# ScalarE copies half of the selected key blocks, VectorE multiplies the copies in place

## The chip, the cores and the metric

One core of one Trainium2 chip runs the kernel. The metric is the device time of one execution in microseconds (us), and less is better. All durations below come from one profiled execution of the kernel before.

## What is computed

One layer of a hybrid decoder is computed for a prompt of 512 positions and, beside it, for 8 decode sequences with one new token each and 4,096 cached positions. The projections, the gated MLP half and the prompt's attention are the large matmul part. The change lies in the decode attention, cut here to what matters (`moba_sample` of the reference):

```
k_full = cache_k[page_table].reshape(Bd, n_full, 256, H, D)     # 16 blocks of 256 keys
kmean  = mean(k_full, axis=2)
gate   = einsum('bhtd,bnhd->bhtn', q, kmean)
_, sel = top_k(gate, 3)                                         # 3 blocks for each head
kg, vg = keys and values of the selected blocks                 # 8 heads x 3 = 24 blocks
s      = einsum('bhtd,bhtkd->bhtk', q, kg) * scale - slope * distance
p      = softmax(s);  out = einsum('bhtk,bhtkd->bhtd', p, vg)
```

Every number is float32.

## The kernel before

**Order.** Each engine executes a list of steps whose order is written at build time by a planner (`make_plan`, line 51). The planner keeps lanes of steps for each engine, with a planned duration and the steps that each depends on, and takes the next step by start time and then by lane rank. Two of its settings matter here. `MARGIN` (line 397) is a hold: on TensorE, a step of the lanes gate, score and spread is planned no earlier than its inputs' planned time plus this hold, so that TensorE gets projection work in front of it. On the chip only the order is left of the plan; each step then waits on semaphores for its real inputs.

**TensorE** (PE) carries the projections of the prompt (line 1036, seven chunks of the input projection; line 1142, the output projection), the prompt attention (lines 1090 to 1120) and, put between them, the small decode steps: `gs` (line 1159) sums the key rows of four blocks, `bc`, `mt` and `mb` (lines 1166, 1171, 1175) spread numbers over partitions, `pv0` and `pv1` (line 1188) multiply probabilities by values.

**One decode sequence b (batch), 8 in a row.**
- GpSimd (POOL) issues 16 gathers of key blocks from the cache into the tile K (line 899), with up to 5 in flight. K holds exactly one sequence. So the first gather of sequence b+1 (line 973) waits until the selected blocks of b have been taken out of K.
- VectorE (DVE) adds the two rows of each block (`ks`, line 744) and TensorE sums them (`gs`).
- VectorE computes the block scores and the top three (`ga`, lines 1572 to 1589).
- `ex` (lines 1608 to 1628) is split in PARTS = 4 parts of 6 instructions. Each instruction reads one 128x128 piece of K (one head's two halves of one block, at an address that comes from registers loaded from selT), multiplies it by q (tile qb), and writes it to kq, which lies in the tile ksum. The last one signals `s_ext`.
- `pg` (lines 1590 to 1607) looks up the page numbers and signals `s_sel`. It stands behind the first part of `ex`, for the last sequence ahead of all of them.
- `sr` (line 1634) reduces kq over the head dimension to scores and signals `s_scr`.
- `bc`, `mt`, `mb` add distances, take the maximum and exponentiate (ScalarE, line 1356), then TensorE executes `pv0` and `pv1`.
- The values V are fetched by SyncE's queue (SP) and by POOL's behind the 16 key gathers of b+1, for the last sequence by SP, POOL and ScalarE's queue (line 729, called by line 1353). All of these fetches wait for `s_sel`.
- SP spreads q of the next sequence over the partitions into qb (line 824), after `s_ext`.

**ScalarE** (ACT) evacuates the projections from PSUM (line 1302), does the exponentials (line 1339) and the copies of transposed probabilities (line 1347) of the prompt attention, sums of squares (line 1237), the copies behind `pv` (lines 1382 and 1383), and issues the weight loads (line 655). It does nothing with K.

## Time and profile before

| What | Value |
|---|---|
| Time, median of 3 runs | 459.38 us (459.01 to 478.45) |
| Time of the profiled execution | 457.99 us |
| Its span in the profile | 456.4 us |
| PE busy | 402.1 us (88%) |
| DVE busy | 278.8 us (61%) |
| POOL busy | 244.7 us (54%) |
| ACT busy | 125.2 us (27%) |

The span runs from the first to the last record of the profile; the time has 1.6 us more around it. PE's busy time includes the waiting of pipelined matmuls behind one another, so 88% says that it is seldom without work, not that it is at its peak. An engine's idle time costs something only where another engine, or the end, waits for it.

### The profile page before, as it was taken

To read this page: it belongs to the slowest core of one execution; us is meant where nothing else is said; L and a number is where in the kernel's file an instruction comes from. 1 tells how busy PE (TensorE), PEld (TensorE's weight loads), DVE (VectorE), ACT (ScalarE), POOL (GpSimd) and SP (SyncE) were. 2 spreads that over 40 slices of the span, in tenths; PEclk is the share of its full clock that TensorE was granted. 3 is DMA by queue.
4 is the path that set the end of the run, shared out by engine and by line. 5 is a ranking of instruction groups with operands and counts; after the bars stand their busy time and mean duration, and the time that the engine had idled before them with its cause. 6 is when DMAs were issued, how large, how long until landed. Compare 5 with 4: busy or idle time off the path is not lost.

```text
span 456.4 us, 8864 instructions
## 1 busy us (share of the span) xinstructions
PE 402.1 (88%) x2696; PEld 189.5 (42%) x2696; DVE 278.8 (61%) x756; ACT 125.2 (27%) x282; POOL 244.7 (54%) x347
## 2 busy tenths in 40 slices
PE   4896997998779999899998897989999388999993
PEld 2543442433343444344553354434443253334433
DVE  2443167447624569666966884868865796567432
ACT  2310120000012223554547522362435401000101
POOL 4776305556446506563377745882566556667121
PEclk9897998999979999899999998999999769999999
DMA  8999158996799936997499849975699599945311
GB/s 223 408 390 337 49 183 227 363 328 164 202 382 331 254 105 190 361 320 185 117 336 318 241 127 333 327 202 156 210 368 337 162 362 378 343 103 117 115 46 52
DMA packets 79695, 111.26 MB, mean 244 GB/s; under 512 B 46560, under 2 KB 47584, under 8 KB 79648
## 3 DMA queue, kind: packets, MB, share of 16 engines
q0 software_dynamic: 22576, 71.45, 46.4%
q1 hardware_dynamic: 45280, 21.26, 18.3%
q10 hardware_dynamic: 11792, 17.98, 13.2%
q8 instruction: 22, 0.36, 0.3%
q14 instruction: 25, 0.20, 0.1%
HBM read 106.34 MB, written 4.29 MB: 242 GB/s over the span
## 4 chain that ended last, share of the span: by engine, by line
PE 27%; DMA 25%; issue 13%; POOL 10%; DVE 9%; SPq 7%; another core or an unknown queue 4%; DVEq 2%; POOLq 2%; ACT 1%
DMA K<-in_cache_k,kidx 20%; PE PA L1036 12%; POOL K L899 8%; PE PA L1142 7%; SPq L777 4%; DVE ksum L1619 4%; DMA V<-in_cache_v 2%; PE SB L990 2%; PE GB L1159 2%; DMA V<-in_page_table 2%; PE DC L1188 1%; DVEq L1617 1%; POOLq L726 1%; SPq L780 1%
## 5 line engine op out<-in xcount | busy, mean ns | idle before, releaser
L899 POOL DMA_INDIRECT K<-in_cache_k,kidx x128 | 135.5, 1059 | 135.3 <-DVE ksum L1619 69.2
L1036 PE MATMUL PA<-wbuf,hT 128*128 128x512 f32 x384 | 187.8, 623 | 4.5 <-ACT vn L1302 2.6
L744 DVE TENSOR_TENSOR ksum<-K 128x512 f32<-128x512 f32 x128 | 86.5, 689 | 74.7 <-DMA K<-in_cache_k,kidx 54.4
L1036 PEld LDWEIGHTS PA<-wbuf,hT 128*128 128x128 f32 x384 | 69.4, 196 | 82.1 <-issue 73.3
L729 POOL DMA_DIRECT2D V<-in_cache_v x128 | 76.2, 595 | 33.8 <-issue 26.1
L1142 PE MATMUL PA<-wbuf,hT 128*128 128x512 f32 x128 | 59.6, 606 | 0.0
L1619 DVE TENSOR_TENSOR ksum<-K,qb 128x128 f32<-128x128 f32 x192 | 41.8, 287 | 10.9 <-issue 4.3
L1159 PE MATMUL GB<-ksum,win 128*32 128x512 f32 x256 | 34.1, 604 | 5.0 <-DVE ksum L744 4.7
L1142 PEld LDWEIGHTS PA<-wbuf,hT 128*128 128x128 f32 x128 | 23.1, 192 | 25.7 <-issue 25.2
L1036 PE MATMUL PA<-hT,wbuf 128*128 128x512 f32 x64 | 31.0, 630 | 0.0
L990 PE MATMUL SB<-wbuf,hTs 128*32 128x128 f32 x576 | 22.0, 305 | 6.7 <-DMA wbuf<-in_w_in 3.7
L1634 DVE TENSOR_REDUCE sc<-ksum 128x48 f32<-128x3072 f32 x8 | 26.8, 3352 | 0.2
L1339 ACT ACTIVATE pr<-pr,smax 128x128 f32<-128x128 f32 (+3 forms) x32 | 18.0, 561 | 31.8 <-DVE smax L1518 20.6
L990 PEld LDWEIGHTS SB<-wbuf,hTs 128*32 128x32 f32 x576 | 18.4, 123 | 12.0 <-issue 7.0
L1515 DVE SCALAR_TENSOR_TENSOR pr<-alibi,SB 128x128 f32<-128x128 f32 (+3 forms) x32 | 15.4, 482 | 11.2 <-PE SB L1090 10.1
L912 POOL TENSOR_SCALAR rstd<-msum 128x1 f32<-128x1 f32 (+1 forms) x18 | 4.8, 268 | 26.7 <-DVE msum L1545 20.0
L1302 ACT ACT_TABLE_LOAD x13 | 16.7, 1283 | 8.2 <-PE PA L1036 6.6
L1188 PE MATMUL DC<-V,pex 128*32 128x64 f32 x768 | 15.5, 229 | 3.2 <-DMA V<-in_cache_v 2.8
L1347 ACT COPY pT<-SB 128x128 f32<-128x128 f32 (+3 forms) x32 | 12.8, 422 | 19.3 <-PE SB L1099 12.7
L1036 PEld LDWEIGHTS PA<-hT,wbuf 128*128 128x128 f32 x64 | 12.1, 199 | 14.4 <-issue 14.4
L1237 ACT ACTIVATE junk<-PA 128x512 bf16<-128x512 f32 x8 | 4.8, 595 | 45.4 <-PE PA L1142 39.1
L1518 DVE TENSOR_REDUCE smax<-pr 128x1 f32<-128x128 f32 (+3 forms) x32 | 15.6, 486 | 1.1
(200 smaller groups left out, 363.5 us busy)
## 6 DMA issues: line engine op xcount, KB each, us to landing
wbuf<-in_w_in ACTq DMA_DIRECT2D x20, 512.0 KB
V<-in_cache_v SPq DMA_DIRECT2D x240, 32.0 KB
V<-in_cache_v POOLq DMA_DIRECT2D x128, 32.0 KB, 2.8
wbuf<-in_w_out ACTq DMA_DIRECT2D x8, 512.0 KB
wbuf<-in_w_in SPq DMA_DIRECT2D x8, 256.0 KB, 8.6
K<-in_cache_k,kidx POOLq DMA_INDIRECT x128, 7.8
wbuf<-in_w_in SPq DMA_DIRECT2D x4, 512.0 KB
qb<-q_rows SPq DMA_DIRECT2D x8, 256.0 KB
```

What stands on the lines that cost most here:

```text
L729: eng.dma_start(V[j * ROWS:(j + 1) * ROWS, h * TOP + k, :, :], v_pages[bass.ds(page, 1), :, :, h * HD:(h + 1) * HD] .rearrange("a p r d -> ...
L744: eng.tensor_tensor(ksum[:, n % SUMS, :], K[:, n, 0, :], K[:, n, 1, :], ALU.add).then_inc(s_dsum, 1)
L777: sp.dma_start(dst, src, allow_slow_non_contiguous=True).then_inc(s_small, 16)
L899: pool.indirect_dma_start(K[:, n, :, :].rearrange("p r w -> p (r w)"), None, k_rows, bass.IndirectOffsetOnAxis(ap=kidx[:, b, n:n + 1], axis=0)
L990: last = pe.matmul(bank[32 * j:32 * j + 32, :], hTs[:, kc, :], w[:, kc, j * P:(j + 1) * P], start=(kc == 0), stop=(kc == KC - 1), tile_pos ...
L1036: last = pe.matmul(bank[:, :], lhs, rhs, start=(kc == 0), stop=(kc == KC - 1))
L1142: last = pe.matmul(bank[:, :], hT[:, kc, t * P:(t + 1) * P], wbuf[:, c % 2, kc, :], start=(kc == 0), stop=(kc == KC - 1))
L1159: last = pe.matmul(GB[32 * j:32 * j + 32, :], win[:, 31 - g:63 - g], ksum[:, (4 * g + j) % SUMS, :], start=(g == 0), stop=(g == G - 1), ti ...
L1188: last = pe.matmul(DC[32 * j:32 * j + 32, hh * HD:(hh + 1) * HD], pex[:, h, i, r:r + 1].broadcast_to([P, 32]), V[:, h * TOP + i, r, :], st ...
L1339: act.activation(pr[:, a % 2, 0:(i + 1) * P], pr[:, a % 2, 0:(i + 1) * P], ACT.Exp, bias=smax[:, a % 2:a % 2 + 1], accum_out=ssum[:, h, i: ...
L1619: last = dve.tensor_tensor(kq[:, h * TOP + k, :, :], K[:, bass.ds(n, 1), :, h * HD:(h + 1) * HD] .rearrange("p a r d -> p (a r) d"), qb[:, ...
L1634: dve.tensor_reduce(sc[:, :, :, :].rearrange("p h k r -> p (h k) r"), kq[:, :, :, :], AX.X, ALU.add).then_inc(s_scr, 1)
```

## The change

For every sequence, the pieces are numbered x = 8k + h (k the rank of the block, h the head). The first 12 (`BY_ACT`: rank 0 of all heads and rank 1 of heads 0 to 3) are now taken out of K by ScalarE, as plain copies into kq. The other 12 are taken by VectorE as before, in four parts of 3. Then a new VectorE step `em` multiplies the copied pieces by q in place, in two instructions (8 pieces and 4 pieces). `sr` waits for it. The next sequence's gathers wait for VectorE's pieces and ScalarE's copies; the spread of q waits for `em` too. ScalarE's copies start after `s_sel`, so behind `pg`. In the planner they have the first lane of ScalarE and a planned duration of 4.9 us, `ex` goes from 1.7 to 0.9 for a part, `em` gets 1.9, and MARGIN goes from 0.6 to 1.0.

```diff
-PARTS = 4
+PARTS, BY_ACT = 4, 12
...
-("ACT", "weight square score exp turn sample side evacuate squares fetch"),
+("ACT", "copyk weight square score exp turn sample side evacuate squares fetch"),
...
-            deps = [("DVE", ("ex", b - 1, PARTS - 1))] if b else []
+            deps = [("DVE", ("ex", b - 1, PARTS - 1)), ("ACT", ("ex", b - 1))] if b else []
...
-        for s in ([("pg", b)] + parts if b == B - 1 else parts[:1] + [("pg", b)] + parts[1:]) + [("sr", b)]:
+        for s in ([("pg", b)] + parts if b == B - 1 else parts[:1] + [("pg", b)] + parts[1:]) + [("em", b), ("sr", b)]:
             deps = [("ACT", ("mb", b - 1))] if s[0] == "sr" and b else []
-            add("DVE", "gate", s, {"ex": 1.7, "pg": 1.2, "sr": 3.4}[s[0]], *deps)
+            if s[0] == "em":
+                deps.append(("ACT", ("ex", b)))
+            add("DVE", "gate", s, {"ex": 0.9, "pg": 1.2, "em": 1.9, "sr": 3.4}[s[0]], *deps)
+        add("ACT", "copyk", ("ex", b), 4.9, ("DVE", ("pg", b)))
         if b:
-            add("SP", "spread", ("qb", b), 3.0, ("DVE", ("ex", b - 1, PARTS - 1)))
+            add("SP", "spread", ("qb", b), 3.0, ("DVE", ("em", b - 1)))
...
-TILE_US, KEY_US, LAG, MARGIN, SLACK, QUARTERS = 7.4, 1.65, 0.25, 0.6, 0.05, 8
+TILE_US, KEY_US, LAG, MARGIN, SLACK, QUARTERS = 7.4, 1.65, 0.25, 1.0, 0.05, 8
...
                         sp.wait_ge(s_ext, b)
+                        sp.wait_ge(s_exm, b)
...
                         pool.wait_ge(s_ext, b)
+                        pool.wait_ge(s_exa, b)
...
+                elif kind == "ex":
+                    b = s[1]
+                    act.wait_ge(s_sel, b + 1)
+                    if b >= 1:
+                        act.wait_ge(s_scr, b)
+                    for x in range(BY_ACT):
+                        k, h = divmod(x, H)
+                        if h == 0:
+                            block_regs = [act.alloc_register(f"ablk{b}_{k}_{i}") for i in range(H)]
+                            act.load(block_regs, selT[k:k + 1, b % 2, 0:H])
+                        n = act.snap(block_regs[h], min_val=0, max_val=NB - 1)
+                        last = act.copy(kq[:, h * TOP + k, :, :],
+                                        K[:, bass.ds(n, 1), :, h * HD:(h + 1) * HD].rearrange("p a r d -> p (a r) d"))
...
+                    last.then_inc(s_exa, 1)
...
-                    size = H * TOP // PARTS
-                    for x in range(size * part, size * (part + 1)):
+                    size = (H * TOP - BY_ACT) // PARTS
+                    for x in range(BY_ACT + size * part, BY_ACT + size * (part + 1)):
...
+                elif kind == "em":
+                    b = s[1]
+                    dve.wait_ge(s_exa, b + 1)
+                    by_rank = kq[:, :, :, :].rearrange("p (h k) r d -> p k h r d", k=TOP)
+                    q_heads = qb[:, :].rearrange("p (h d) -> p h d", h=H)
+                    for k in range(-(-BY_ACT // H)):
+                        hs = min(H, BY_ACT - k * H)
+                        last = dve.tensor_tensor(by_rank[:, k, 0:hs, :, :], by_rank[:, k, 0:hs, :, :],
+                                                 q_heads[:, 0:hs, :].unsqueeze(2).broadcast_to([P, hs, 2, HD]),
+                                                 ALU.mult)
+                    last.then_inc(s_exm, 1)
                 elif kind == "sr":
                     b = s[1]
                     dve.wait_ge(s_ext, b + 1)
+                    dve.wait_ge(s_exm, b + 1)
```

## Rows read from the trace of the kernel before

**Rows 1.** The page: busy time of each engine, and the chain by line.

```profile
PE 402.1 (88%) x2696; PEld 189.5 (42%) x2696; DVE 278.8 (61%) x756; ACT 125.2 (27%) x282; POOL 244.7 (54%) x347
...
DMA K<-in_cache_k,kidx 20%; PE PA L1036 12%; POOL K L899 8%; PE PA L1142 7%; SPq L777 4%; DVE ksum L1619 4%; DMA V<-in_cache_v 2%; PE SB L990 2%; PE GB L1159 2%; DMA V<-in_page_table 2%; PE DC L1188 1%; DVEq L1617 1%; POOLq L726 1%; SPq L780 1%
```

**Rows 2.** Windows of 15 us: busy us, (instructions), then PEclk, DMA share, GB/s.

```profile
360.00:375.00 15.00, 8.43 (x73) 6.12 (x74) 13.89 (x40) 3.05 (x10) 7.59 (x8) 0.59 0.88 306
...
420.00:435.00 15.00, 15.00 (x132) 6.88 (x131) 6.20 (x18) 2.22 (x9) 3.15 (x7) 1.00 0.36 103
```

**Rows 3.** Waits of POOL and PE: who waited for whom, total us, times, longest.

```profile
POOL K L899 <- DVE ksum L1619: 69.2, 7, 19.9
...
PE DC L1183 <- DMA V<-in_cache_v: 5.0, 1, 5.0
PE GB L1159 <- DVE ksum L744: 4.7, 7, 1.3
...
PE SB L1128 <- DVE yb L1471: 2.3, 1, 2.3
```

**Rows 4.** Timeline of sequence 1: start, us, engine, line, what.

```profile
111.52 1.30 DVE L1619 TENSOR_TENSOR ksum<-K,qb 128x128 f32<-128x128 f32 x6 [0.79 <-DVE selT L1589]
...
113.87 0.20 DVE L1607 STREAM_TRANSPOSE selT<-selw 32x32 int32<-32x32 int32 x1
...
114.23 0.49 DVE L1619 TENSOR_TENSOR ksum<-K,qb 128x128 f32<-128x128 f32 x2 [0.16 <-DVE selT L1607]
...
115.17 3.55 DVE L1619 TENSOR_TENSOR ksum<-K,qb 128x128 f32<-128x128 f32 x16 [0.45 <-issue]
...
118.75 3.35 DVE L1634 TENSOR_REDUCE sc<-ksum 128x48 f32<-128x3072 f32 x1
...
118.99 1.01 POOL L899 DMA_INDIRECT K<-in_cache_k,kidx  x1 [6.55 <-DVE ksum L1619]
...
129.41 0.68 DVE L744 TENSOR_TENSOR ksum<-K 128x512 f32<-128x512 f32 x1
```

**Rows 5.** Timeline of the last sequence: from selection to ScalarE's value fetches and `pv1`.

```profile
408.30 0.20 DVE L1607 STREAM_TRANSPOSE selT<-selw 32x32 int32<-32x32 int32 x1
...
409.46 6.41 ACTq L729 DMA_DIRECT2D V<-in_cache_v  x8
...
416.85 6.14 ACTq L729 DMA_DIRECT2D V<-in_cache_v  x8
...
431.23 0.86 PE L1188 MATMUL DC<-V,pex 128*32 128x64 f32 x46
```

**Rows 6.** Timeline of ACT: small copies from PSUM; small activations that read SBUF.

```profile
155.66 0.43 ACT L1347 COPY pT<-SB 128x128 f32<-128x128 f32 x2 [1.57 <-PE SB L1099]
...
218.16 0.31 ACT L1237 ACTIVATE junk<-vn 128x128 bf16<-128x128 f32 x1
218.38 0.19 ACT L1237 ACTIVATION_READ_ACCUMULATOR junk<-vn 128x1 f32 x1
```

**Rows 7.** DVE by form: count, busy us, mean ns, idle before.

```profile
L744 DVE TENSOR_TENSOR ksum<-K 128x512 f32<-128x512 f32 x128 | 86.5, 689 | 74.7 <-DMA K<-in_cache_k,kidx 54.4 <-PE GB L1159 13.6 <-issue 4.4
```

**Rows 8.** Timeline at 367 us: POOL's gathers beside VectorE's two-input instructions.

```profile
367.66 1.35 POOL L899 DMA_INDIRECT K<-in_cache_k,kidx  x1 [3.07 <-DVE ksum L1619]
369.31 1.56 POOL L899 DMA_INDIRECT K<-in_cache_k,kidx  x1 [0.30 <-issue]
371.18 0.94 POOL L899 DMA_INDIRECT K<-in_cache_k,kidx  x1 [0.30 <-issue]
...
367.29 2.73 DVE L1471 SCALAR_TENSOR_TENSOR yb<-yb,rstd,vn 128x512 f32<-128x512 f32 x4
```

**Rows 9.** Timeline: what ACT and PE do around the selections of sequences 4 and 6.

```profile
267.80 1.28 ACT L1302 ACT_TABLE_LOAD   x1 [5.77 <-PE PA L1036]
...
362.34 0.63 ACT L1237 ACTIVATE junk<-yb 128x512 bf16<-128x512 f32 x1
...
364.30 0.17 PE L1183 MATMUL DC<-psm,one 128*1 128x8 f32 x1 [4.95 <-DMA V<-in_cache_v]
```

More of the change, by code:

```diff
@@ L63, in add @@
         needs[eng, s] = deps
-    for eng, names in (("PE", "gate score first attention side sample project"), ("ACT", "weight square score exp turn sample side evacuate squares fetch"),
+    for eng, names in (("PE", "gate score first attention side sample project"), ("ACT", "copyk weight square score exp turn sample side evacuate squares fetch"),
                        ("DVE", "first " + DVE_LANES), ("POOL", POOL_LANES), ("SP", "spread rows fetch gather"),
@@ L592, in hymba_kernel @@
         s_scr = sem("selected_k_scored")
+        s_exa = sem("selected_k_copied")
+        s_exm = sem("copied_k_times_q")
         s_mxr = sem("decode_max_ready")
@@ L1353, in _ @@
                     fetch_v(act, b, hh, [k], "va")
+                elif kind == "ex":
[11 more added lines that the diff above has]
+                                        K[:, bass.ds(n, 1), :, h * HD:(h + 1) * HD].rearrange("p a r d -> p (a r) d"))
+                        if h == H - 1 or x == BY_ACT - 1:
+                            for r in block_regs:
+                                act.free_register(r)
+                    last.then_inc(s_exa, 1)
                 elif kind == "mb":
@@ L1611, in _ @@
                         dve.wait_ge(s_sel, b + 1)
-                    size = H * TOP // PARTS
-                    for x in range(size * part, size * (part + 1)):
+                    size = (H * TOP - BY_ACT) // PARTS
+                    for x in range(BY_ACT + size * part, BY_ACT + size * (part + 1)):
                         k, h = divmod(x, H)
-                        if h == 0:
+                        if h == 0 or x == BY_ACT:
                             block_regs = [dve.alloc_register(f"blk{b}_{k}_{i}") for i in range(H)]
```

## The prediction

> **What bounds the kernel now.** I read the page first, then the windows, then the waits, then the timelines around the selections. The page shows two strands [rows 1]. TensorE is busy 402.1 of 456.4 us, and the chain that ended last runs through the key gathers (20% on their DMAs, 8% on POOL's issues) and the projections (12% and 7%), in turns. Neither bounds the kernel alone. The waits show why the change aims where it does [rows 3]: POOL stood 69.2 us in 7 waits for VectorE's last extraction, the longest 19.9 us. K has a single copy, so each of these 7 waits ends in a gather that can't start earlier, and it takes from 118.99 to 129.41 us until VectorE adds its first block [rows 4]. An earlier release moves the whole next sequence. But TensorE waits little for it: 4.7 us in 7 waits for key sums, 5.0 us once for values [rows 3]. And after the last selection at 408.3 us TensorE is filled with output projection (15.00 of 15 us in the window from 420) [rows 2, 5]. So a microsecond gained on the key loop isn't a microsecond at the end. It comes out only as far as it takes idle time off TensorE, which has some 54 us of it (456.4 - 402.1), much at the two ends. The fattest place in the middle is the window from 360: 8.43 of 15 us busy, clock granted 0.59 [rows 2].
>
> **Release of K, today.** In sequence 1 the first 6 pieces take 1.30 us, `pg` ends at 114.07 (113.87 + 0.20), and 2 and 16 more pieces end at 118.72: 4.65 us after the selection is ready [rows 4]. A piece costs 1.30 / 6 = 0.217 us.
>
> **Release of K, after.**
> - The part ahead of `pg` falls from 6 to 3 pieces: 3 x 0.217 = 0.65 us earlier for everything behind it, values included (not in the last sequence, where `pg` stands first).
> - VectorE's rest: 9 pieces and one register load. The first piece came 0.16 us after `pg`, and the register load cost 0.45 us [rows 4]: 0.16 + 0.45 + 9 x 0.217 = 2.6 us after the selection. So ScalarE sets the release.
> - ScalarE's start: in the last sequence its queue's first instruction came at 409.46, 0.96 us after the selection at 408.50, with the same loads of 8 registers from selT [rows 5].
> - Twelve copies: the trace has no ScalarE instruction on K. Bounds: two copies of this size from PSUM took 0.43 us, 0.215 each; an activation that reads 128x128 from SBUF takes 0.31 us, and the engine took its next instruction 0.22 us after its start [rows 6]. Low end 12 x 0.215 = 2.6, high end, nothing overlapped, 12 x 0.31 = 3.7. I take 11 x 0.22 + 0.31 = 2.7, since this row reads SBUF as the copies do. The second register load adds 0 to 0.45 us; I take 0.45.
> - Sum: 0.96 + 2.7 + 0.45 = 4.1 us after the selection (3.6 to 5.1), against 4.65. With the 0.65, the release is 1.2 us earlier (0.2 to 1.7).
>
> *A rule on small operands.* The activation's duration is 0.31 us [rows 6]. The Trainium skill (VectorE: DVE Perf Modes, section The TRN2 errata) gives a ScalarE instruction with SBUF source 224 + 128 = 352 cycles of 1.2 GHz, 0.29 us, and advises tiles of 512 elements and more, which speaks against twelve copies of 128. The duration agrees with the trace; if the fixed part lay bare between all of them, an estimate from that page is 12 x 0.29 = 3.5 us, a release 4.9 us after the selection, and a gain of 0.4 us instead of 1.2.
>
> **What eats at the 1.2 us.** (a) ScalarE is in order. At the selection of sequence 4 it is idle (until 267.80), near that of sequence 6 it is in squares until 362.97 [rows 9]. I take 0.3 us on the mean. (b) `em` now runs beside POOL's first gather. It has two SBUF inputs. Beside four such instructions of VectorE two gathers took 1.35 and 1.56 us, alone the next took 0.94 [rows 8]. `em` ends after about 1.8 us, so it covers one and a bit: +0.4 us (0 to 1.0, for both). Today `sr`, with one input, stands there, and the gather took 1.01 [rows 4]. Left: 1.2 - 0.3 - 0.4 = 0.5 us for each of 7 handovers, 3.5 us by the last sequence (-8 to +12 from the bounds).
>
> *The port rule.* The gather beside two-input work took 1.35 us against 0.94 [rows 8]. The Trainium skill (SBUF — State Buffer, section SBUF: two separate sides) says that VectorE with two SBUF inputs and a GpSimd operation that reads SBUF exclude each other for the whole instruction. The trace shows a slower gather, not one held for all of 2.73 us.
>
> (c) MARGIN grows by 0.4, so TensorE's last `gs` of each sequence is put up to 0.4 us later. The planned release is 6.8 + 1.2 = 8.0 us behind `ga` today and 0.9 + 1.2 + 0.25 + 4.9 = 7.25 after. In the order TensorE's steps thus move 0.35 us earlier for each sequence while the real release moves 0.5: TensorE should wait less for key sums.
>
> **The score path.** 8 pieces are 1024 columns, 4 are 512. A 512-column instruction of this kind takes 0.689 us [rows 7]; two of these bound the first, 1.38 us, less about 0.1 to 0.2 for one start instead of two: `em` 1.2 + 0.7 = 1.9 us. `sr` then ends 4.1 + 0.1 + 1.9 + 3.35 = 9.45 us after the selection, today 4.65 + 3.35 = 8.0 [rows 4]. With 0.65 off it's 0.8 us later. Behind the waiting `em` on VectorE stand `sr`, then maxima of the prompt attention and `bc`. The next key sums are no victim: the first came at 129.41, 7 us after `sr` ended at 122.1 [rows 4]. The plan counts the path 1.4 us longer, so TensorE's order allows for it: cost 0, and up to 5 x 0.8 = 4 us if the five sequences beside the attention aren't covered. VectorE's own load: -12 x 0.217 + 1.9 = -0.7 us per sequence, on an engine busy 61% [rows 1]: 0. SP's spread of q is needed a whole loading phase later: 0.
>
> **The last sequence.** ScalarE copies before it issues its two value fetches, which took 6.41 and 6.14 us from 409.46 and 416.85 [rows 5]. The start moves by 4.1 - 0.96 = 3.1 us, so the second ends near 426 instead of 423, and `pv1` uses the values at 431.23 [rows 5]: hidden by the 5 us, less the landing. Without that cover, one for one.
>
> **The sum at the end.** TensorE's 7 waits for key sums hold 4.7 us; with 0.4 more hold each I take off 7 x 0.4 = 2.8. Its 4.95 us for values at 359 to 364 [rows 9] shrink with the earlier key phase, since POOL fetches those values behind the gathers: real minus planned shift is 6 x (0.5 - 0.35) = 0.9. Against that, near sequence 6 the squares that open the way to the output projection (TensorE waited 2.3 us for it [rows 3]) may stand behind ScalarE's copies: 0 or 3.1 us, I take 0.7. Net -2.8 - 0.9 + 0.7 = -3.0. The profiled execution took 457.99 us (span 456.4 and 1.6 around it), so 455.0; the median of the runs is 1.4 above this execution, so **456**.
>
> **The rivals.**
> - *No gain at the end, 458 to 462.* Copies at their high bound and ScalarE late by half a microsecond leave -0.6 us per handover. For it: TensorE is full behind the last selection. Chance 0.21. In it lies the port rule in full: `em`'s longer instruction holding every first gather costs 1.2 - 0.4 = 0.8 more on each of 7, 455 + 6 = 461. Against: only 0.4 is seen [rows 8]. Chance 0.05 of its own.
> - *Slower, 467 to 476.* ScalarE's copies block the prompt attention. Its exponentials, copies and evacuations stand behind a wait for the selection, and TensorE's order has them at planned times. Each microsecond by which the selection is later on the chip than in the plan, beyond the softness of two PSUM banks, is TensorE idle in sequences 2 to 6: 5 x 2 to 3.5 us = 10 to 17, and the clock falls as at 360 (0.59) [rows 2]. It decides from about 2 us lateness on. Against: VectorE, in order too, waits at the same places today. Chance 0.16.
> - *A large gain, 445 to 450.* The order of TensorE around 358 to 372 comes out free of its waits: 5.0 for values and 2.3 for `yb` [rows 3] and the slow clock, with the 2.8: some 10 us. Chance 0.16.
> - The forecast, 452 to 458: 0.42.
>
> **How the numbers follow.** The likeliest gives 456. About 2% either way (450.2 and 468.6) is what a measurement of this kernel can tell. Faster by more: the large gain, 0.16. Slower by more: most of the blocking case, 0.13. Within: 0.71. The range 447 to 467 leaves out about 0.07 below and 0.13 above.
>
> **What would show it.** The copies 0.20 to 0.24 us apart, from about 1 us behind the selection; the first gather 4.1 us behind it and 1.2 to 1.5 us long; POOL's wait now for ScalarE's line; PE's waits for key sums below 3 us; PE busy again near 402. Copies 0.3 us apart, PE waiting for `pr` or `pT` of ScalarE by more than 5 us, or the key loop shorter by 7 us and more with an end that follows it, would make the prediction wrong.

## The result: 5.4% slower

The changed kernel took 488.27 us (median of 4 runs, 484.39 to 493.04), the kernel before beside it 460.03 us (median of 4 runs). The ratio is 1.054, with a 95% interval from 1.049 to 1.059. The profiled execution took 484.61 us, its span is 483.0. All ratios in this document are of executions whose clock was not disturbed, a median is of all runs, and the profiled executions of e2, e4, e5, e7, e8, e9, e11 and e17 were among the disturbed, longer ones.

Busy time by engine and the group of ScalarE's copies, from the page of the changed kernel (its line numbers are shifted: 1372 is ScalarE's copies, 1643 VectorE's pieces, 1660 `em`, 1670 `sr`, 905 the key gathers, 749 `ks`, 1166 `gs`, 1195 `pv`, 997 the projections of the new tokens):

```profile
PE 409.8 (85%) x2696; PEld 194.0 (40%) x2696; DVE 272.8 (56%) x676; ACT 139.5 (29%) x374; POOL 244.5 (51%) x347
...
L1372 ACT COPY ksum<-K 128x128 f32 x96 | 20.1, 294 | 33.8 <-DVE selT L1631 33.6
```

Waits of the changed kernel (who waited for whom, us in total, times, longest):

```profile
POOL K L905 <- ACT ksum L1372: 75.5, 6, 21.3
...
PE DC L1195 <- issue: 10.1, 13, 1.3
PE SB L997 <- DMA wbuf<-in_w_in: 7.3, 1, 7.3
PE DC L1062 <- ACT junk L1244: 6.8, 2, 6.1
PE PA L1043 <- ACT vn L1309: 6.3, 1, 6.3
...
PE GB L1166 <- DVE ksum L749: 1.5, 2, 1.0
```

TensorE is busy 7.7 us more than in [rows 1] and idle 18.9 us more (73.2 against 54.3). The wait for key sums shrank from 4.7 us [rows 3] to 1.5, as forecast. In its place stand waits that were shorter before: 10.1 us of "issue" between small matmuls of `pv` (before 0.4), 7.3 for weights (3.7), 6.1 at the end (0.8) and 6.3 for `vn` (2.6).

The handover itself went nearly as predicted. Timeline of sequence 1 in the changed kernel:

```profile
111.46 0.20 DVE L1631 STREAM_TRANSPOSE selT<-selw 32x32 int32<-32x32 int32 x1
...
112.58 2.09 ACT L1372 COPY ksum<-K 128x128 f32 x10 [1.63 <-DVE selT L1631]
112.66 1.71 DVE L1643 TENSOR_TENSOR ksum<-K,qb 128x128 f32<-128x128 f32 x8 [0.54 <-issue]
...
114.58 0.49 ACT L1372 COPY ksum<-K 128x128 f32 x2
115.10 1.83 DVE L1660 TENSOR_TENSOR ksum<-ksum,qb 128x1024 f32<-128x1024 f32 x2 [0.74 <-ACT ksum L1372]
115.86 1.35 POOL L905 DMA_INDIRECT K<-in_cache_k,kidx  x1 [7.42 <-ACT ksum L1372]
...
117.02 3.35 DVE L1670 TENSOR_REDUCE sc<-ksum 128x48 f32<-128x3072 f32 x1
```

The selection is ready at 111.66, the last copy ends at 115.07 (3.4 us later), the gather starts at 115.86 (4.2 later; before, 118.99 - 114.07 = 4.9 [rows 4]). So the handover gained, and the span lost 26.6 us (483.0 - 456.4). What follows is about that difference.

A table from the timelines helps to see where. Ahead of the first selection the first keys are loaded. Between the first selection and the last (seven sequences) the time divides into three: selection to first gather, start of the first to start of the last gather (the loading phase), and last gather to the next selection (landing, last additions and `gs`, block scores). The tail is from the last selection to the end.

| profiled execution | to first selection | selection to gather | loading phases | last gather to selection | tail | TensorE idle in the loading phases |
|---|---|---|---|---|---|---|
| before | 66.0 | 35.0 | 175.6 | 131.9 | 47.9 | 18.0 |
| changed | 62.2 | 32.3 | 194.2 | 142.6 | 51.7 | 34.8 |
| e3, new work, old order | 61.3 | 30.0 | 182.5 | 134.6 | 48.3 | 20.6 |
| e17, before, 4 in flight | 59.4 | 35.0 | 204.4 | 121.2 | 49.4 | 27.0 |
| e18, changed, 4 in flight | 60.4 | 33.3 | 203.7 | 112.6 | 51.5 | 18.7 |
| e15, before, 3 in flight | 65.1 | 35.0 | 233.2 | 109.0 | 48.4 | 29.7 |
| e16, changed, 3 in flight | 63.9 | 32.2 | 236.2 | 109.9 | 50.8 | 28.3 |
| e5, half gathers, 5 in flight | 59.5 | 35.0 | 145.4 | 220.8 | 47.6 | 40.9 |
| e13, half gathers, 2 in flight | 69.8 | 35.0 | 229.0 | 99.0 | 51.2 | 22.4 |

Of the 18.9 us that TensorE is idle more in the changed kernel, 16.8 come in the loading phases (34.8 against 18.0) and 7.7 in the tail (15.4 against 7.7), while the rest of the span has 5.6 less.

### The profile page after: what moved, and what is told of

Read it like the earlier page. It is cut to its first block and busy times, and to the rows that moved or that the text cites. A ratio compares the mean times of both kernels' runs of the same rounds, so it can differ in the third digit from the quotient of the medians.

```text
span 483.0 us, 8906 instructions
## 1 busy us (share of the span) xinstructions
PE 409.8 (85%) x2696; PEld 194.0 (40%) x2696; DVE 272.8 (56%) x676; ACT 139.5 (29%) x374; POOL 244.5 (51%) x347
## 5 line engine op out<-in xcount | busy, mean ns | idle before, releaser
L749 DVE TENSOR_TENSOR ksum<-K 128x512 f32<-128x512 f32 x128 | 85.9, 687 | 59.4 <-DMA K<-in_cache_k,kidx 46.0
L997 PE MATMUL SB<-wbuf,hTs 128*32 128x128 f32 x576 | 27.5, 331 | 12.9 <-DMA wbuf<-in_w_in 7.3
L1372 ACT COPY ksum<-K 128x128 f32 x96 | 20.1, 294 | 33.8 <-DVE selT L1631 33.6
L997 PEld LDWEIGHTS SB<-wbuf,hTs 128*32 128x32 f32 x576 | 21.6, 134 | 20.1 <-issue 10.5
L1043 PE MATMUL PA<-hT,wbuf 128*128 128x512 f32 x64 | 29.6, 602 | 0.0
L1195 PE MATMUL DC<-V,pex 128*32 128x64 f32 x768 | 17.7, 221 | 13.4 <-issue 10.1
L1643 DVE TENSOR_TENSOR ksum<-K,qb 128x128 f32<-128x128 f32 x96 | 21.7, 287 | 11.4 <-DVE selT L1613 4.8
L1195 PEld LDWEIGHTS DC<-V,pex 128*32 128x32 f32 x768 | 13.3, 109 | 19.8 <-issue 19.7
L1354 ACT COPY pT<-SB 128x128 f32<-128x128 f32 (+3 forms) x32 | 13.1, 423 | 27.5 <-PE SB L1106 16.8
L1675 DVE TENSOR_TENSOR sbias<-DC,slope 128x24 f32<-128x24 f32 x8 | 1.4, 181 | 34.1 <-PE DC L1173 18.9
L1539 DVE SCALAR_TENSOR_TENSOR pr<-alibi,SB 128x128 f32<-128x128 f32 (+3 forms) x32 | 15.4, 481 | 6.8 <-PE SB L1097 6.7
L1043 PEld LDWEIGHTS PA<-hT,wbuf 128*128 128x128 f32 x64 | 11.4, 190 | 13.8 <-issue 13.7
```

Of the source, the lines that this page charges most:

```text
L749: eng.tensor_tensor(ksum[:, n % SUMS, :], K[:, n, 0, :], K[:, n, 1, :], ALU.add).then_inc(s_dsum, 1)
L997: last = pe.matmul(bank[32 * j:32 * j + 32, :], hTs[:, kc, :], w[:, kc, j * P:(j + 1) * P], start=(kc == 0), stop=(kc == KC - 1), tile_pos ...
L1043: last = pe.matmul(bank[:, :], lhs, rhs, start=(kc == 0), stop=(kc == KC - 1))
L1195: last = pe.matmul(DC[32 * j:32 * j + 32, hh * HD:(hh + 1) * HD], pex[:, h, i, r:r + 1].broadcast_to([P, 32]), V[:, h * TOP + i, r, :], st ...
L1372: last = act.copy(kq[:, h * TOP + k, :, :], K[:, bass.ds(n, 1), :, h * HD:(h + 1) * HD].rearrange("p a r d -> p (a r) d"))
L1643: last = dve.tensor_tensor(kq[:, h * TOP + k, :, :], K[:, bass.ds(n, 1), :, h * HD:(h + 1) * HD] .rearrange("p a r d -> p (a r) d"), qb[:, ...
```

## The experiments

### The order against the work: e1 to e4 and e8

The change does two things at once. It moves work from VectorE to ScalarE, and through MARGIN and new planned durations it makes the planner write another order: 140 of TensorE's 465 steps stand elsewhere. e3 gives the planner the old numbers and the new steps no duration, so that all engines keep the old order with the new steps put in (on SyncE, one spread of q and one fetch change places). e4 keeps the new order and does the old work in it.

**e1**, MARGIN alone, in the kernel before:

```diff
-TILE_US, KEY_US, LAG, MARGIN, SLACK, QUARTERS = 7.4, 1.65, 0.25, 0.6, 0.05, 8
+TILE_US, KEY_US, LAG, MARGIN, SLACK, QUARTERS = 7.4, 1.65, 0.25, 1.0, 0.05, 8
```

> The kernel before with MARGIN 1.0 instead of 0.6; no other edit, so only the order of steps changes. The changed kernel took 488.27 us against 460.03 (ratio 1.054). Theory O (the order that the planner writes is what costs the time, and the hold is the part of it that counts): 475 us or more. Theory W (the new work itself, ScalarE's copies and VectorE's second pass, costs it): 460, within 1% of before. A third reading, O2 (the order counts, but through the planned durations of the new steps): also near 460 here.

Measured 466.86 us (461.63 to 476.79), ratio 1.016 (0.997 to 1.036). It moved 137 of TensorE's steps, and its loss can't be told from none. Theory O, which put the loss on the hold, wanted 475 or more.

**e2**, the changed kernel with the old MARGIN of 0.6:

> The changed kernel with MARGIN back at 0.6. Theory O (hold): 460 or less. Theory W (the work): stays near 488. O2 (any new order is a draw of its own): anywhere from 460 to 500, with other waits of TensorE than in the changed kernel.

Measured 499.28 us (495.04 to 514.25), ratio 1.084 (1.065 to 1.104): worse than the changed kernel. MARGIN 1.0 isn't what made the changed kernel slow.

**e3**, the new work in the old order:

```diff
-TILE_US, KEY_US, LAG, MARGIN, SLACK, QUARTERS = 7.4, 1.65, 0.25, 1.0, 0.05, 8
+TILE_US, KEY_US, LAG, MARGIN, SLACK, QUARTERS = 7.4, 1.65, 0.25, 0.6, 0.05, 8
-            add("DVE", "gate", s, {"ex": 0.9, "pg": 1.2, "em": 1.9, "sr": 3.4}[s[0]], *deps)
+            add("DVE", "gate", s, {"ex": 1.7, "pg": 1.2, "em": 0.0, "sr": 3.4}[s[0]], *deps)
-        add("ACT", "copyk", ("ex", b), 4.9, ("DVE", ("pg", b)))
+        add("ACT", "copyk", ("ex", b), 0.0, ("DVE", ("pg", b)))
```

> The changed kernel's work in the order of before: the planner gets MARGIN 0.6, 1.7 us for each part of VectorE's extraction and 0.0 for ScalarE's copies and VectorE's second pass, which leaves the order of TensorE, ScalarE, VectorE and GpSimd exactly that of before with the new steps put in. Theory W (the work costs it): 485 to 490, as in the changed kernel. Theory O (the order costs it): 452 to 460, that is what was predicted for the work, with the key release after the selection at some 3.5 us against 4.65.

Measured 461.06 us (453.52 to 466.83); the kernel before beside it 463.46.

**e4**, the old work in the new order: the changed kernel, in which `range(BY_ACT)` of the copies and the range of `em` are empty, VectorE takes all 24 pieces, and the waits for `s_exa` and `s_exm` and those of ScalarE's copy step are gone.

> The order of the changed kernel with the work of before: VectorE takes all 24 pieces with q, ScalarE's copy step and VectorE's second pass issue nothing, and their waits are gone. Theory W: back at 460. Theory O: 480 or more, since the order stays. If the work helps and the order harms, this one is the slowest of the four, some 3 to 7 us above the changed kernel.

Measured 484.52 us (477.95 to 488.28), ratio 1.046 (1.024 to 1.068). Busy time on the two pages, first e3, then e4:

```profile
PE 402.9 (88%) x2696; PEld 188.4 (41%) x2696; DVE 272.6 (60%) x676; ACT 144.3 (32%) x378; POOL 244.6 (54%) x347
```

```profile
PE 411.8 (85%) x2696; PEld 194.2 (40%) x2696; DVE 277.3 (57%) x756; ACT 119.2 (24%) x278; POOL 242.2 (50%) x347
```

**e8**, e3 once more with more runs:

> The new work in the old order once more, in 5 rounds, for an interval. Seven handovers of K, each some 0.9 us earlier after the selection. If the gain came through in full: 453 to 455 (ratio 0.985). If TensorE's fixed order swallows it: within 0.5% of before.

Measured 466.40 us (458.79 to 474.68, 12 runs), ratio 1.015 (1.003 to 1.026).

The four corners: old work, old order 460 to 463; new work, old order 461 to 466; old work, new order 485; new work, new order 488. TensorE's busy time points the same way (402.1 and 402.9 against 409.8 and 411.8), but says less: in e8, the same kernel as e3, it is 407.1. **The order costs some 21 to 27 us, the work 0 to 1.5%.** That the handover's gain didn't come through shows in e3's row of the table: 5.0 us less from selection to gather, 6.9 us more in the loading phases and 2.7 more behind them.

### Is it this order, or any other? e7, e9 and e10

**e7** and **e9** change one planned duration of the kernel before by 0.1 us. Every instruction is the same, and 122 and 110 steps of TensorE move.

```diff
-            add("DVE", "gate", s, {"ex": 1.7, "pg": 1.2, "sr": 3.4}[s[0]], *deps)
+            add("DVE", "gate", s, {"ex": 1.8, "pg": 1.2, "sr": 3.4}[s[0]], *deps)
```

> The kernel before with one planned duration changed: 1.8 instead of 1.7 us for each part of the extraction. The same instructions on every engine, in another order (122 of TensorE's 465 steps move). If the order of before is a lucky or tuned draw, and any other costs: 470 to 490. If only the order that came with the change is bad: 456 to 466.

Measured 477.49 us (469.68 to 478.08); the kernel before beside it 462.82.

> The kernel before, in which only the planner's duration of one part of ex goes from 1.7 to 1.6 us; every instruction is the same, and 110 of TensorE's 465 steps stand elsewhere. Theory O (the order that the kernel before has is a good draw, and any plan that differs moves some hundred steps and loses what that draw had): slower, 466 to 485 us where the kernel before is near 460, ratio 1.015 to 1.05. Rival P (what costs is a longer plan for the handover, as in the changed kernel, where the planned release moved; a plan with a shorter part is no loss): ratio 0.99 to 1.01.

Measured 485.84 us (475.47 to 486.69); before beside it 463.02. Neither run has an interval. Lowest against lowest, e7 stands 3.9% above the kernel before beside it (469.68 against 452.03) and e9 4.5% (475.47 against 454.99). Shorter or longer, both lose, so it isn't the direction in which the planned release moved. Nor does every other order lose: e1 moved 137 steps and lost nothing that can be measured.

**e10** gives the changed kernel's planner what its trace shows:

```diff
-            add("DVE", "gate", s, {"ex": 0.9, "pg": 1.2, "em": 1.9, "sr": 3.4}[s[0]], *deps)
+            add("DVE", "gate", s, {"ex": 0.7, "pg": 1.2, "em": 1.9, "sr": 3.4}[s[0]], *deps)
-        add("ACT", "copyk", ("ex", b), 4.9, ("DVE", ("pg", b)))
+        add("ACT", "copyk", ("ex", b), 3.2, ("DVE", ("pg", b)))
```

> The changed kernel, in which the planner gets the durations that its trace shows: 3.2 us for ScalarE's copies instead of 4.9, 0.7 for a part of ex instead of 0.9, MARGIN 1.0 as it was. Theory O (the order is a draw; truer durations by a microsecond or two are no cure, since the plan doesn't know what the chip loses): 470 to 495 us, with no reason to lie below the changed kernel's 485 by more than the spread between draws (some 10 us). Rival T (the order is bad because the plan holds the copies to be 1.7 us longer than they are): back to 458 to 465.

Measured 483.51 us (478.81 to 487.26), ratio 1.061 (1.048 to 1.074). Truer durations are no cure.

Does the plan know? In part. Its own end is 425.9 us for the kernel before and 427.3 for e1, 432.2 for e7, 437.3 for e2, 442.8 for e9: the last three are longer in the plan too. But it holds the changed kernel at 427.9 and e10 at 425.9, and these two should have taken what the kernel before takes, not 24 to 28 us more. Something that the plan doesn't hold hits these orders.

### What hits them: pauses and late signals beside the gathers

In the changed kernel the loading phase of sequence 4 takes 37.2 us (before 25.3). There matmuls of `pv` come singly, with gathers of POOL between them. The timeline of the changed kernel:

```profile
224.52 0.99 PE L1195 MATMUL DC<-V,pex 128*32 128x64 f32 x38
...
224.86 0.93 POOL L905 DMA_INDIRECT K<-in_cache_k,kidx  x1 [0.30 <-issue]
...
226.09 0.94 POOL L905 DMA_INDIRECT K<-in_cache_k,kidx  x1 [0.30 <-issue]
226.67 0.27 PE L1195 MATMUL DC<-V,pex 128*32 128x64 f32 x2 [1.16 <-issue]
...
227.34 0.94 POOL L905 DMA_INDIRECT K<-in_cache_k,kidx  x1 [0.30 <-issue]
...
228.18 0.22 PE L1195 MATMUL DC<-V,pex 128*32 128x64 f32 x1 [1.24 <-issue]
228.58 0.93 POOL L905 DMA_INDIRECT K<-in_cache_k,kidx  x1 [0.30 <-issue]
...
230.34 0.26 PE L1195 MATMUL DC<-V,pex 128*32 128x64 f32 x1 [1.22 <-issue]
...
237.63 0.15 ACT L1406 COPY denr<-DC 1x8 f32<-1x8 f32 x1 [9.64 <-remote]
```

38 matmuls take 0.99 us together, and the next eight take 9.2 us. "issue" says that the profile shows nothing they wait for. Their last one ended at 234.7, and ScalarE's copy of the result started at 237.63.

Signals come late too. In the same kernel, three transposes of `pr` (line 1106) end at 288.72, and ScalarE's copy of them starts at 297.15, after 7.3 us of idle time that ends with a signal ("remote"); POOL issues gathers until 296.25; a spread (line 1173) ends at 293.34 and VectorE's `sbias` starts at 297.30. TensorE then waited 6.35 us for `vn`, which stood behind that copy:

```profile
288.23 0.49 PE L1106 MATMUL SB<-ident,pr 128*128 128x128 f32 x3
...
292.94 0.40 PE L1173 MATMUL DC<-spread,one 8*128 8x24 f32 x2
...
297.15 0.48 ACT L1354 COPY pT<-SB 128x384 f32<-128x384 f32 x1 [7.30 <-remote]
297.30 0.18 DVE L1675 TENSOR_TENSOR sbias<-DC,slope 128x24 f32<-128x24 f32 x1 [5.80 <-remote]
...
299.68 2.08 PE L1043 MATMUL PA<-wbuf,hT 128*128 128x512 f32 x2 [6.35 <-ACT vn L1309]
```

The ends of matmuls are modelled in these profiles, so it isn't told apart whether the signal was late or the matmul itself.

It isn't new. In the kernel before the copy at 183.90 us starts 2.9 us behind its transposes, with POOL at its gathers until 182.55:

```profile
180.50 0.49 PE L1099 MATMUL SB<-ident,pr 128*128 128x128 f32 x3
...
181.61 0.94 POOL L899 DMA_INDIRECT K<-in_cache_k,kidx  x1 [0.30 <-issue]
...
183.90 0.86 ACT L1347 COPY pT<-SB 128x384 f32<-128x384 f32 x2 [4.49 <-remote]
```

How much of the loss is this? TensorE's idle time in the loading phases sorts all the orders that ran with full gathers and five in flight. It is 18.0 to 22.5 us in the four executions whose spans are 456.4 to 464.9 (before 18.0, e1 19.9, e3 20.6, e8 22.5) and 34.0 to 55.3 us in the seven with spans of 476.3 to 512.5 (e7 34.0, changed 34.8, e9 37.5, e4 37.7, e10 42.6, e11 43.8, e2 55.3; e11 is the changed kernel with shifted code, further down). Not all of it is of the kind shown here: in the changed kernel "issue" makes 13.8 us of it (before 5.5) and the wait for `vn` 6.3. The 7.3 us for weights were not traced to a cause, nor was the longer idle time in the tail.

**e5 and e6: half the bytes.** The first guess was the DMA load. In both orders each gather brings 2 KB instead of 4 KB for a partition (of every pair of rows the second is left out and replaced by the first; this holds for all "half gathers" kernels).

```diff
-                    pool.indirect_dma_start(K[:, n, :, :].rearrange("p r w -> p (r w)"), None, k_rows,
+                    pool.indirect_dma_start(K[:, n, 0, :], None, k_half,
```

> The kernel before with each key gather halved: one row of 2 KB for each partition instead of 4 KB, and the one row is used in both places (so the second row of every pair of keys is left out). The partner of the next kernel. The DMA engines carry some 33 of 111 MB less, so the long stretches in which they are full shrink. Both theories: faster than before, 440 to 455, if only because the gathers land sooner; TensorE's own work is unchanged at some 400 us.

> The order of the changed kernel with the work of before (the run that took 484.52 us), with the same halved gathers. With full gathers the new order costs 21 us over the old one. Theory D (the new order puts bursts of small matmuls and late weight loads into stretches in which the DMA engines are full, and there TensorE trickles): the difference to the old order with halved gathers falls below 8 us, and the pauses of 1.2 us between small matmuls near 225 to 240 us go. Theory S (TensorE waits in that order for steps of the other engines, whatever the DMAs do): the difference stays at 15 us or more, and the tail after the last selection stays 4 us longer.

e6 is e4 with the same edit. Measured 505.37 us (old order) and 527.84 us (new order). The difference of 22 us stayed, where the theory of the load wanted less than 8. And both lost over 40 us with fewer bytes to move, which no theory had. The table tells where: loading phases 30 us shorter, the rest up to the selection 89 us longer. The gathers now land so soon that POOL hardly waits for one (1.9 us in 2 waits) and issues up to 16 in one row, in the kernel before up to 7. Windows of e5 over two such stretches (busy us of PE, PEld, DVE, ACT, POOL, then clock, DMA share, GB/s):

```profile
187.30:206.00 18.70, 8.45 (x29) 3.60 (x25) 6.33 (x16) 3.33 (x8) 14.41 (x15) 0.74 0.70 230
299.90:319.80 19.90, 8.51 (x56) 3.97 (x55) 6.98 (x11) 2.93 (x6) 15.33 (x17) 0.73 0.84 241
```

TensorE, VectorE and ScalarE are each busy for less than half of the time, with the DMA engines below their full share. Counting every stretch of four and more gathers with less than 0.45 us between them: in the kernel before they make 82 us, with TensorE idle for 10.0 of them; in e5 149 us, with 46.5 idle. TensorE's idle time between its first and last matmul grew by 36 us (43.4 to 79.3), as much as the idle time in these stretches did. For the kernels of this case the count doesn't decide: the changed one has 96 us of such stretches, up to 8 gathers in a row, with only 9.1 us idle. Its pauses from 228.9 to 234.4 us lie beside gathers 0.6 to 0.8 us apart, and beside other work of POOL.

**e11 and e12: shifted code.** Another reason could be that TensorE runs out of fetched code in rows of small matmuls. 128 waits that are fulfilled at once, ahead of its first step, shift the code:

```diff
-            pe.wait_ge(s_ident, 1)
+            for _ in range(128):
+                pe.wait_ge(s_ident, 1)
```

> The changed kernel with 128 more waits, all fulfilled at once, ahead of TensorE's first step, so that each of its instructions lies 128 places later in its code. The pauses in question (before, TensorE's 3,267th to 3,270th instruction; changed, its 2,486th to 2,498th, lone small matmuls some 1.2 us apart, after a code page was fetched at 224.0 us and before the next at 246.6) are explained by theory F as TensorE running out of fetched code in a row of small instructions while the queues are full of gathers: then they move to other instructions, some 128 earlier, or are gone, and the key phase of sequence 4 (37.2 us from its first to its last gather) is 28 to 33 us. Rival G (those matmuls wait for something else that goes with the place in the work, a port or a bank): the pauses stay at the same matmuls and the key phase at 36 to 38. Time 480 to 490 by G, 475 to 485 by F, in both with up to 6 us more if the extra waits aren't hidden by the first loads.

> The kernel before with half gathers (each gather brings one row of each pair, the second is left out and replaced by the first) and the same 128 waits ahead of TensorE's first step. There the pauses were longest: eight and more of 0.7 to 2.1 us in the 32 small matmuls of L991 (TensorE's 3,267th to 3,282nd), 306 to 323 us. Theory F: at other instructions, some 128 earlier, or gone; 485 to 505 us. Rival G: at the same matmuls, 500 to 512 us.

Measured 497.62 us (2 runs) and 509.61 us (1 run). The code pages were fetched up to 159 instructions earlier, but around the pauses in question only 4 and 21 earlier in e11, and 84 and 116 in e12, so e12 is the firmer of the two. The pauses of 0.7 us and more stayed with their matmuls: in the changed kernel they stand at its 1,238th to 1,245th matmul (weight loads not counted), in e11 at the 1,237th to 1,243rd, still `pv1` of the same sequence (phase 37.4 us); in half gathers at the 1,634th to 1,642nd in e5 and the 1,634th to 1,643rd in e12. No code page was fetched during them (in the changed kernel at 224.0 us and then at 246.6). Theory F falls for these pauses. (e12 also had three at the 366th to 369th matmul, where e5 had one at the 396th.)

**e13 and e14: POOL's unbroken issue, or SyncE's fetches beside it?**

```diff
-                    if n >= FLIGHT:
-                        pool.wait_ge(s_k[n - FLIGHT], 16 * (b + 1))
+                    if n >= 2:
+                        pool.wait_ge(s_k[n - 2], 16 * (b + 1))
```

> The kernel before with half gathers (the second row of each pair is left out and replaced by the first), and POOL waits for the landing of the gather but one before instead of the fifth before, so that it can't issue gathers one behind the other. Instructions and their order are those of e5, which took 505 us, and in whose unbroken stretches of four and more gathers TensorE stood idle 46.5 us of 149, against 10.0 of 82 in the kernel before. Theory U (TensorE, SyncE and the signals between engines are held up while POOL issues gathers without a break): the idle time in those stretches falls below 15 us, and the time to 465 to 485 although each loading phase gets longer. Rival S (SyncE's value fetches hold TensorE up, whatever POOL does): pauses of 0.7 us and more stay beside the fetches, 495 to 515 us.

Measured 485.83 us (1 run), just above theory U's range and 20 less than e5, with the same instructions in the same order and each gather held back longer. No stretch of four is left, and single matmuls are gone but for one pause of 0.46 us: the pauses that remain are waits for named inputs, or ahead of a new step. A reader sees the breaks in e13's timeline of POOL:

```profile
301.79 1.28 POOL L900 DMA_INDIRECT K<-in_cache_k,kidx  x1 [1.80 <-DMA K<-in_cache_k,kidx]
303.37 0.96 POOL L900 DMA_INDIRECT K<-in_cache_k,kidx  x1 [0.30 <-issue]
306.02 1.28 POOL L900 DMA_INDIRECT K<-in_cache_k,kidx  x1 [1.69 <-DMA K<-in_cache_k,kidx]
```

Then the other way round, SyncE's fetches held back and POOL left alone:

```diff
                     sp.wait_ge(s_sel, b + 1)
+                    if b + 1 < B:
+                        sp.wait_ge(s_k[NB - 1], 16 * (b + 2))
```

> The kernel before with half gathers (second row left out, as in e5), and SyncE fetches a sequence's values only when the next sequence's 16 gathers have landed. POOL issues its gathers unbroken as in e5. Theory U: lone matmuls 1.2 us apart are still there beside unbroken gathers. Rival S: no such pause in a stretch of gathers without fetches of SyncE (below 5 us of idle in them beside waits that name what they wait for), a gather stretch of 16 costs TensorE nothing, while waits for values come on top, so the time itself tells less: 500 to 540 us by both.

Measured 517.93 us (1 run). Its timeline has SyncE's last DMA issue ending at 298.93 (296.45 + 2.48), and the single matmuls behind it:

```profile
296.45 2.48 SPq L839 DMA_DIRECT2D obs<-osb  x4
...
302.69 0.95 POOL L902 DMA_INDIRECT K<-in_cache_k,kidx  x1 [0.30 <-issue]
303.56 0.27 PE L1191 MATMUL DC<-V,pex 128*32 128x64 f32 x1 [1.05 <-issue]
303.94 0.95 POOL L902 DMA_INDIRECT K<-in_cache_k,kidx  x1 [0.30 <-issue]
...
305.19 0.95 POOL L902 DMA_INDIRECT K<-in_cache_k,kidx  x1 [0.30 <-issue]
305.71 0.27 PE L1191 MATMUL DC<-V,pex 128*32 128x64 f32 x1 [1.02 <-issue]
```

From 299 to 306 us the gathers' queue takes 79.6% of the DMA engines' time, and all other queues 1.7%. So a row of POOL's gathers with five in flight is enough, and rival S falls.

**e15 to e18: the same cure for the two kernels of this case**, by the edit of e13 with 3 and with 4 instead of 2. The plan and every engine's order stay as they are.

> The kernel before, same plan and order, in which POOL waits for the landing of the third gather before instead of the fifth: shorter unbroken stretches, 3 in flight. Theory U: the pauses in its gather stretches (10.0 us in all) mostly go, but the loading phase may get longer (24 to 29 us today, DMA share about 1 in it): 452 to 463 us. Rival S: nothing gained, the loading phase longer, 460 to 480.

> The changed kernel, same plan and order, with the wait for the third gather before. Theory U: the pauses of 225 to 243 us are gone and the loading phase of sequence 4 falls from 37.2 to 24 to 30 us; 470 to 482. Rival S: they stay, 482 to 500.

Measured 491.49 us (ratio 1.066, 1.053 to 1.080) and 494.17 us (1.071, 1.054 to 1.088). Both missed theory U's time: the loading phases grew by 58 and 42 us in all, and their price was larger than the pauses' worth. e16's 494 lies in the range of rival S, but the pauses that S wanted to stay are gone: between matmuls of one step none is longer than 0.52 us in e15 and 0.46 in e16. And the two orders now take the same. As the phases may have covered everything, four in flight was tried as the step between.

> The kernel before, same plan and order, POOL waits for the landing of the fourth gather before instead of the fifth. With three in flight it took 491 us, the loading phases 32 to 36 us instead of 24 to 29. Theory L (the loading phase sets the time of this order): phases of 27 to 31 us and 465 to 478 us. Rival (the pauses are worth as much as the longer phase): 455 to 464.

> The changed kernel with the wait for the fourth gather before. It took 488 us with five in flight and 494 with three. Theory M (the new order's loss shrinks as POOL's unbroken stretches do): phases of 27 to 31 us, no phase of 37, 476 to 488 us, within 2.5% of e17. Rival N (the order loses the same whatever POOL does, and with three in flight was only covered): 488 to 500, over 4% above e17.

Measured 463.71 us (ratio 1.023, 1.011 to 1.035) and **462.56 us** (460.04 to 463.89; ratio 1.018, 1.005 to 1.032). With one gather less in flight the changed kernel stands 1.8% above the kernel before instead of 5.4% (462.56 against 488.27 us), below the range of both theories, and the order that cost some 25 us costs nothing: e17 and e18 differ by 0.2%. The kernel before lost a little by the same edit, and its 464 lies in the rival's range: theory L, which let the longer phases (29.2 us on the mean) set the time, wanted 465 or more. The late signals shown above are gone: here are the same instructions of e18.

```profile
271.87 0.49 PE L1106 MATMUL SB<-ident,pr 128*128 128x128 f32 x3
...
273.76 0.48 ACT L1354 COPY pT<-SB 128x384 f32<-128x384 f32 x1 [0.73 <-PE SB L1106]
...
276.59 0.40 PE L1173 MATMUL DC<-spread,one 8*128 8x24 f32 x2
...
277.02 0.18 DVE L1675 TENSOR_TENSOR sbias<-DC,slope 128x24 f32<-128x24 f32 x1 [1.43 <-PE DC L1173]
```

`sbias` starts 0.03 us behind its spread instead of 3.96. In all, the waits of ScalarE and VectorE that end with "remote" fall from 75.8 us in 13 waits to 37.0 in 7 (before 36.0 in 9). The pauses between matmuls of one step are shorter, but not gone: the `pv1` in the loading phase of sequence 4 still has six, and its last seven matmuls take 4.4 us, where the last eight took 9.2.

```profile
219.20 0.22 PE L1195 MATMUL DC<-V,pex 128*32 128x64 f32 x1 [0.45 <-issue]
...
222.92 0.22 PE L1195 MATMUL DC<-V,pex 128*32 128x64 f32 x1 [0.51 <-issue]
```

Pauses of 0.7 us and more within a step number 2 in the kernel before, 8 in the changed one, 11 in e5 and 10 in e14, and none in e13 and e15 to e18. In the table the changed kernel pays 9.5 us in the loading phases for four in flight and gets back 30.0 us between last gather and selection. TensorE's idle time in the loading phases falls from 34.8 to 18.7 us, which is 16.1 of the 21.3 us by which the span shrinks. That in the tail stays (16.4 us). The place where `pv1` trickled (20 us around it in the changed kernel, then in e18; same columns as above):

```profile
225.00:245.00 20.00, 10.09 (x102) 6.46 (x91) 5.94 (x5) 6.91 (x19) 11.95 (x13) 0.69 1.01 344
```

```profile
211.00:231.00 20.00, 15.96 (x189) 9.00 (x188) 12.20 (x22) 12.22 (x37) 10.44 (x12) 0.91 0.79 246
```

The granted clock of 0.69 in the first is a mean over its two levels, 1.2 and 2.4 GHz: it was at the lower from 229 to 239 us, behind the single matmuls, which makes the pause dearer than its length.

No version ran that beats the kernel before by more than can be measured: e3, e17 and e18 lie within 2.5% of it.

## Why the prediction was wrong, point by point

- **The release** was forecast 4.1 us behind the selection (3.6 to 5.1) and came at 3.2 to 3.4 (first copy at 0.7 to 0.9, forecast 0.96), with the gather at 4.0 to 4.3 in five of seven handovers of e3 and in six of the changed kernel. The copies were 0.20 us apart, and the second register load cost nothing. In the changed kernel's seventh handover VectorE's pieces were the late ones (gather 7.6 us behind), behind other work of its new order. Part of the gain was lost at a term that the sum lacked: POOL started 0.28 us behind VectorE's last piece before, and 0.79 us behind ScalarE's last copy. The Trainium skill's rule (VectorE: DVE Perf Modes, section The TRN2 errata) gave 0.29 us for a copy, and the trace has 294 ns; but its copies overlap, so the estimate of 3.5 us for twelve was too high by 1.
- **ScalarE in order** was priced at 0.3 us per handover. In the old order it cost 1.0 us once (e3, sequence 3) and 0.5 once. The rival of the copies blocking the prompt attention named the right side and at most 16 of the 28 us (467 to 476 against 488), and it is wrong: e4 has no copies and is as slow, e3 has all of them and isn't.
- **`em` beside the gather**: forecast +0.4 us, found +0.35 in sequence 1 (1.35 against 1.01). In four of the changed kernel's seven handovers `em` came later and the gather took 1.00 to 1.11 us, in the seventh it took 2.44. `em` takes 1.83 us (forecast 1.9). The port paragraph set the slower gather of [rows 8] against 2.73 us, which are four instructions. The hold is for single instructions, as the last section shows.
- **`sr` ends later**: forecast 9.45 us behind the selection. In e3 8.5 to 9.5 in six of seven; in the new order 10.7 to 11.0 in three. No loss can be traced to it.
- **The last sequence** was hidden as forecast: the tail of e3, which has the copies, is 48.3 us against 47.9. The changed kernel's 51.7 belongs to its order, for e4 has 51.4 without a copy.
- **TensorE's waits for key sums** fell from 4.7 to 1.5 us, forecast below 3. The step was right and worth nothing, since the time went elsewhere.
- **The step that failed** put the new order at nothing. It is in the paragraph on MARGIN and in "the plan counts the path 1.4 us longer, so TensorE's order allows for it: cost 0". I priced the new plan by how far planned and real releases move against each other, a shift of some tenths per sequence. But a plan is a list of 465 steps, of which 140 moved, and no step of the sum priced that. e4 shows the price of the list alone: 21 us. It appears as idle time of TensorE in the loading phases (34.8 us against 18.0) and in the tail (15.4 against 7.7). With one gather less in flight the idle time in the loading phases is 18.7 us, and both orders take the same (e17 and e18). TensorE's busy time was forecast near 402 and came at 409.8. The range ended at 467 because all its terms were sized from the work.
- **The forecast for the work alone** wasn't far off: 456 against e3's 461.1 and e8's 466.4. Its gain of 3 us isn't there: e8's ratio is 1.003 to 1.026.

The late signals weren't in the prediction, though the row was in the trace of before: ScalarE's copy at 183.90 us, ended by "remote" with its input long complete. An idle time that no input explains should have been followed up.

## What to carry to other kernels

When an edit also feeds a planner, separate the two before believing either: the new work in the old order and the old work in the new order are two kernels, and here they told all of the loss from none. An order that was found by trying is worth something only together with what it was tried with, so a change of a planned 0.1 us can cost 3 to 5%. And try fewer indirect DMAs in flight beside small instructions of other engines: with one gather less, a bad order took as long as the tuned one.

## What the runs showed that I had not expected

- **While POOL issued gathers one behind the other** (0.95 us each, 0.30 apart), small matmuls of one step came singly, with pauses of 0.5 to 2.5 us, and ScalarE and VectorE saw TensorE's signals up to 8.4 us late. Half the bytes in each gather made it worse (46.5 us of TensorE idle in such stretches against 10.0), since POOL then hardly paused. Three and two in flight took it away, four made it shorter. Why it is so stays open: a pause with five in flight wasn't tried, so the number in flight and the breaks aren't told apart, nor what TensorE's instructions and signals share with POOL's gathers. In e5, TensorE and ScalarE came back at 203.6 us while POOL issued until 206.0, so a break of POOL isn't always what ends it.
- **A gather beside two-input work of VectorE** took 1.35 us in sequence 1 and 2.44 us in sequence 6 of the changed kernel. The latter ends 0.99 us behind `em`, and a gather of the kernel before that starts in a `ks` addition ends 0.81 us behind it (376.29 + 1.27 against 376.06 + 0.69):

```profile
390.94 1.82 DVE L1660 TENSOR_TENSOR ksum<-ksum,qb 128x1024 f32<-128x1024 f32 x2
391.31 2.44 POOL L905 DMA_INDIRECT K<-in_cache_k,kidx  x1 [7.57 <-DVE ksum L1643]
```

```profile
376.06 0.69 DVE L744 TENSOR_TENSOR ksum<-K 128x512 f32<-128x512 f32 x1 [0.21 <-DMA K<-in_cache_k,kidx]
376.29 1.27 POOL L899 DMA_INDIRECT K<-in_cache_k,kidx  x1 [1.68 <-DMA K<-in_cache_k,kidx]
```

  Of the 46 gathers of the kernel before that start in such an addition with over 0.2 us of it left, 45 end 0.79 to 0.85 us behind its end, or behind that of another addition directly following. The gather of sequence 1 fits too: the first of `em`'s two instructions ends at 116.32 us (115.10 + 1.22), and the gather 0.89 us later. So these gathers were held until one or two instructions of VectorE had ended, and then took another 0.8 to 1.0 us. That agrees with the Trainium skill (SBUF — State Buffer, section SBUF: two separate sides), by which the two exclude each other for the whole instruction.
- **A signal from ScalarE costs POOL more**: POOL starts 0.5 us later behind ScalarE's last copy than behind VectorE's last piece (0.79 against 0.28), in nearly every handover of every kernel here. It isn't the second wait: where VectorE's piece came last in the changed kernel, POOL started 0.29 us behind it.
